# A two-block network on one core: latent norm moved forward, indexer slots in rotation, weight splits three ahead, a shorter inverse root, first gate group as whole fp32 products

## What is computed

```
h = rmsnorm(x, norm1_g[l])
z = h @ w_in[l]                                  # 2520 columns for four mixers, 4096 for gates
z_mla, z_nsa, z_fox, z_dsa, z_gate = split_cols(z, ...)
o_mla = mla_mixer(z_mla, ...)                    # starts with rmsnorm(c_q), rmsnorm(c_kv): the "latent" norm
o_nsa = nsa_mixer(...); o_fox = fox_mixer(...)
o_dsa = dsa_mixer(...)                           # an indexer scores all keys with 8 heads, top 64 are kept
lifted = einsum('bsnc,ncd->bsnd', stack(o_...), w_branch[l])
gates = sigmoid(z_gate)                          # 1024 -> 4 x 1024
x = x + sum(gates * lifted) @ w_out[l]
x = x + square(relu(rmsnorm(x) @ w_up[l])) @ w_down[l]
```

## Time and profile before

| | us |
|---|---|
| median of 3 runs | 1681.21 (1676.3 to 1685.93) |
| the profiled execution | 1678.43 |
| its span, first to last instruction | 1676.7 |
| TensorE busy | 1550.4 |
| VectorE, ScalarE, GpSimd busy | 821.7, 739.6, 595.2 |

### The profile page before, as it was taken

One profiled execution on the slowest core, in us unless ns is written; L12 is line 12 of the kernel. 1 busy time (PEld: TensorE's weight loads), 2 busy tenths in 40 slices (PEclk: granted clock), 3 DMA queues, 4 the chain that ended last, 5 costly groups with the idle time before them and its releaser, 6 DMA issues.

```text
span 1676.7 us, 23289 instructions
## 1 busy us (share of the span) xinstructions
PE 1550.4 (92%) x9590; PEld 1253.5 (75%) x9590; DVE 821.7 (49%) x1470; ACT 739.6 (44%) x1057; POOL 595.2 (35%) x227
## 2 busy tenths in 40 slices
PE   5999989999997999989889899999998798899997
PEld 4867867875996778578666658999886676589996
DVE  2734578324866764163664463522437733645222
ACT  3334366423436654143445344444434454354442
POOL 1200034320000442135555225655546443246543
PEclk9999889999997999999999999999999899999999
DMA  9597279769625786753343354555443333355550
GB/s 386 196 327 277 87 269 343 267 234 388 264 83 201 254 322 226 279 195 132 106 136 122 103 192 156 196 179 181 169 148 114 116 105 134 132 187 196 192 185 25
DMA packets 51225, 327.22 MB, mean 195 GB/s; under 512 B 5936, under 2 KB 5936, under 8 KB 17456
## 3 DMA queue, kind: packets, MB, share of 16 engines
q1 hardware_dynamic: 51120, 325.73, 53.8%
HBM read 324.66 MB, written 1.05 MB: 194 GB/s over the span
## 4 chain that ended last, share of the span: by engine, by line
PE 75%; DVE 17%; ACT 4%; DMA 2%; issue 1%; POOL 1%; DVEq 0%; SPq 0%; ACTq 0%
PE ps L224 19%; PE ps L225 18%; PE ps L226 18%; PE ps L221 16%; DVE lo L232 4%; DMA raw<-in_wmod 2%; DVE pb L2755 1%; PE ps L2704 1%; ACT hi L229 1%; DVE z L232 1%; DVE s L240 1%; ACT pb L229 1%; POOL lo L232 1%; DVE pb L232 1%; DVE rt L232 1%
## 5 line engine op out<-in xcount | busy, mean ns | idle before, releaser
L232 POOL TENSOR_TENSOR lo<-raw,hi 128x2048 fp32r<-128x2048 f32 (+2 forms) x76 | 354.2, 4670 | 647.4 <-ACT hi L229 647.4
L229 ACT ACTIVATE hi<-raw 128x2048 fp32r<-128x2048 f32 (+2 forms) x192 | 350.5, 1858 | 43.5 <-POOL big L232 16.9
L232 DVE TENSOR_TENSOR lo<-raw,hi 128x2048 fp32r<-128x2048 f32 (+1 forms) x116 | 291.8, 2531 | 97.1 <-ACT hi L229 96.9
L232 POOL TENSOR_TENSOR loh<-rawh,hih 128x1024 fp32r<-128x1024 f32 x64 | 156.0, 2450 | 141.9 <-ACT hih L229 141.6
L224 PE MATMUL ps<-hTh,hi 128*128 128x256 f32 x640 | 182.6, 285 | 5.4 <-DVE hTl L232 2.9
L225 PE MATMUL ps<-hTl,hi 128*128 128x256 f32 x640 | 181.8, 284 | 0.0
L226 PE MATMUL ps<-hTh,lo 128*128 128x256 f32 x640 | 181.7, 284 | 0.0
L224 PEld LDWEIGHTS ps<-hTh,hi 128*128 128x128 f32 x640 | 123.4, 193 | 7.2 <-issue 3.5
L224 PE MATMUL ps<-hi,hTh 128*128 128x512 f32 (+3 forms) x320 | 118.9, 372 | 10.2 <-DVE hTl L232 5.6
L225 PEld LDWEIGHTS ps<-hTl,hi 128*128 128x128 f32 x640 | 123.5, 193 | 0.5
L226 PEld LDWEIGHTS ps<-hTh,lo 128*128 128x128 f32 x640 | 123.5, 193 | 0.0
(11 more groups left out here) (306 smaller groups left out, 2990.1 us busy)
## 6 DMA issues: line engine op xcount, KB each, us to landing
raw<-in_wgu SPq DMA_DIRECT2D x64, 1024.0 KB, 4.9
raw<-in_wmod SPq DMA_DIRECT2D x48, 1024.0 KB, 6.9
raw<-in_wdn SPq DMA_DIRECT2D x32, 1024.0 KB, 5.6
rawh<-in_wgt SPq DMA_DIRECT2D x64, 512.0 KB, 3.8
raw<-in_wup SPq DMA_DIRECT2D x32, 1024.0 KB, 4.8
raw<-in_wdown SPq DMA_DIRECT2D x32, 1024.0 KB, 5.1
raw<-in_wz SPq DMA_DIRECT2D x12, 1024.0 KB, 4.7
raw<-in_wbr SPq DMA_DIRECT2D x8, 1024.0 KB, 4.9
```

The source lines that it names most:

```text
L229: return self.e.activation(o, a, f, **kw)
L232: return self.e.tensor_tensor(o, a, b, op)
```

## The change

Five edits, all in one diff. `v_fill` and `g_fill` change as `a_fill` does.

1. The first gate group (g = 0, four chunks per layer) is no longer split. TensorE multiplies the fp32 weights by the fp32 `hT` directly. The high slots in `hT`'s place become free when these are done.
2. The other gate chunks are split three ahead in place of two. The first two chunks of g = 1 are split at steps i = 1 and 2 of g = 0.
3. The first step of `v_latent` becomes `v_latent_in`, called in `v_indexer` before its first pause. It works in `s1` in place of `s2`.
4. The indexer's slot is `n % 4`, and ScalarE waits for head n - 4.
5. `v_rstd` takes one bit operation and one polynomial: 8 operations in place of 10. `v_stats`, which sums squares first, has them scaled in ScalarE's Square and takes 8 in all in place of 11.

```diff
     def enter_gates(self, l):
-        self.rings["H"] = [NH + i for i in range(4)]
+        self.rings["H"] = [NH + i for i in (2, 3, 0, 1)]
-        self.before["H"][NH:NH + 2] = [None] * 2
+        self.before["H"][NH:NH + 2] = [("used", ("gt", l, 0, 3))] * 2
...
     if name == "gt":
-        return part(t_in["wgt"][at[0], at[1]], at[2], 1024), "pool"
+        return part(t_in["wgt"][at[0], at[1]], at[2], 1024), "pool" if at[1] else "raw"
...
+    ROOT = 0.7235405817547222, -3.722988595072433, 5.6564527047170285, -4.5444396531968065, 2.4630066686385943
     def v_rstd(self, v, dst, ss, inv_n, tmp):
...
+        v.ts(dst.bitcast(I32), ss.bitcast(I32), -0.5, 1597463007.0, ALU.mult, ALU.add).then_inc(*v.up("dve"))
+        v.stt(tmp, dst, scale, dst, ALU.mult, ALU.mult).then_inc(*v.up("dve"))
         v.tt(tmp, tmp, ss, ALU.mult).then_inc(*v.up("dve"))
+        v.stt(ss, tmp, c[0], tmp, ALU.add, ALU.mult).then_inc(*v.up("dve"))
+        for x in c[1:3]:
+            v.stt(ss, ss, x, tmp, ALU.add, ALU.mult).then_inc(*v.up("dve"))
+        v.stt(dst, ss, c[3], dst, ALU.add, ALU.mult).then_inc(*v.up("dve"))
...
     def a_z(self, a, l):
-            if i == 5:
-                for k in range(4):
-                    a.wait_ge(*a.at("hT", ("c", l), k))
-                self.a_split(a, "gt", l, 0, 0, ahead=1)
...
     def t_fill(self, t, l):
                 c = t.chunk("gt", l, g, i)
+                if g:
+                    wh, wl = kn(c.hi, 2), kn(c.lo, 2)
+                    t.wait_ge(*t.at("lo", c.key))
+                else:
+                    t.wait_ge(*t.at("landed", c.key))
...
+                        else:
+                            m = t.mm(self.ps[:, b, :], self.hT[:, 2 * i + k, rows], kn(c.raw, 2)[:, k, :], first, last)
...
     def a_fill(self, a, l):
-                self.a_split(a, "gt", l, g, i, ahead=2)
+                if g:
+                    self.a_split(a, "gt", l, g, i, ahead=3)
+                elif i in (1, 2):
+                    self.a_split(a, "gt", l, 1, i - 1, ahead=0)
...
     def a_indexer(self, a, l):
-                        if n % 2:
-                            a.wait_ge(*a.at("idx head", l, n - 1))
-                        elif n >= 8:
-                            a.wait_ge(*a.at("idx head", l, n - 7))
+                        if n >= 4:
+                            a.wait_ge(*a.at("idx head", l, n - 4))
...
     def v_indexer(self, v, l):
         v.ts(V.wi, self.z[:, :, SM + 16:SM + 24], 8 ** -0.5, None, ALU.mult).then_inc(*v.up("dve"))
+        self.v_latent_in(v, l)
         yield
```

More of the change, by code:

```diff
@@ L101, in leave, with enter_gates @@
         self.before["H"][:NH - 1] = [key] * (NH - 1)
-    def enter_gates(self):
+    def enter_gates(self, l):
         self.epoch += 1
@@ L641, in v_gate @@
         v.mark("grow", l, g, half)
+    ROOT = 0.7235405817547222, -3.722988595072433, 5.6564527047170285, -4.5444396531968065, 2.4630066686385943
     def v_rstd(self, v, dst, ss, inv_n, tmp):
+        scale, *c = self.ROOT
         v.wait_ge(*v.last)
-        v.ts(ss, ss, inv_n, EPS, ALU.mult, ALU.add).then_inc(*v.up("dve"))
+        if inv_n is not None:
+            v.ts(ss, ss, inv_n, EPS, ALU.mult, ALU.add).then_inc(*v.up("dve"))
+            v.wait_ge(*v.last)
+        v.ts(dst.bitcast(I32), ss.bitcast(I32), -0.5, 1597463007.0, ALU.mult, ALU.add).then_inc(*v.up("dve"))
         v.wait_ge(*v.last)
[L650 to L654, removed]
+        v.stt(tmp, dst, scale, dst, ALU.mult, ALU.mult).then_inc(*v.up("dve"))
         v.wait_ge(*v.last)
@@ L657, in v_rstd @@
         v.wait_ge(*v.last)
-        v.stt(dst, tmp, 1.5, dst, ALU.add, ALU.mult).then_inc(*v.up("dve"))
-        c = 0.375 ** 0.5
+        v.stt(ss, tmp, c[0], tmp, ALU.add, ALU.mult).then_inc(*v.up("dve"))
+        for x in c[1:3]:
+            v.wait_ge(*v.last)
+            v.stt(ss, ss, x, tmp, ALU.add, ALU.mult).then_inc(*v.up("dve"))
         v.wait_ge(*v.last)
[L661 to L667, removed]
+        v.stt(dst, ss, c[3], dst, ALU.add, ALU.mult).then_inc(*v.up("dve"))
     def a_stats(self, a, name, src, ready, buf, c0, *freed, halves=(0, 1)):
@@ L676, in a_stats @@
                     a.wait_ge(*a.last)
-                a.ac(buf[:, 0:512], src[:, t, 512 * h:512 * h + 512], ACT.Square,
+                a.ac(buf[:, 0:512], src[:, t, 512 * h:512 * h + 512], ACT.Square, scale=1.0 / 32,
                      accum_out=self.st[:, c0 + 2 * h + t:c0 + 2 * h + t + 1]).then_inc(*a.up("act"))
@@ L684, in v_stats @@
         v.wait_ge(*v.at("squares", name))
-        v.tt(ss, ss, self.st[:, c0 + 2:c0 + 4], ALU.add).then_inc(*v.up("dve"))
-        self.v_rstd(v, self.st[:, c0 + 4:c0 + 6], ss, 1.0 / 1024, self.st[:, c0 + 6:c0 + 8])
+        v.stt(ss, ss, EPS, self.st[:, c0 + 2:c0 + 4], ALU.add, ALU.add).then_inc(*v.up("dve"))
+        self.v_rstd(v, self.st[:, c0 + 4:c0 + 6], ss, None, self.st[:, c0 + 6:c0 + 8])
         v.mark("rstd of", name)
@@ L2202, in t_fill @@
                     for k in range(2):
-                        m = t.mm3(self.ps[:, b, :], [h[:, 2 * i + k, 128 * q:128 * q + 128] for h in self.H3],
-                                  (wh[:, k, :], wl[:, k, :]), i == k == 0, i == 3 and k == 1)
+                        first, last, rows = i == k == 0, i == 3 and k == 1, slice(128 * q, 128 * q + 128)
+                        if g:
+                            m = t.mm3(self.ps[:, b, :], [h[:, 2 * i + k, rows] for h in self.H3],
+                                      (wh[:, k, :], wl[:, k, :]), first, last)
+                        else:
+                            m = t.mm(self.ps[:, b, :], self.hT[:, 2 * i + k, rows], kn(c.raw, 2)[:, k, :], first, last)
                     if i == 3:
@@ L2291, in v_fill @@
             for i in range(4):
-                self.v_split(v, "gt", l, g, i, ahead=2)
+                if g:
+                    self.v_split(v, "gt", l, g, i, ahead=3)
+                elif i in (1, 2):
+                    self.v_split(v, "gt", l, 1, i - 1, ahead=0)
                 yield
@@ L2331, in g_fill @@
             for i in range(4):
-                self.g_split(g, "gt", l, gg, i, ahead=2)
+                if gg:
+                    self.g_split(g, "gt", l, gg, i, ahead=3)
+                elif i in (1, 2):
+                    self.g_split(g, "gt", l, 1, i - 1, ahead=0)
                 yield
@@ L2439, in v_indexer @@
                         h = 4 * i + 2 * j2 + j
-                        r, wcol = s2[:, 256 * (h % 4):256 * (h % 4) + nk], V.wi[:, q, h:h + 1]
+                        r, wcol = s2[:, 256 * (n % 4):256 * (n % 4) + nk], V.wi[:, q, h:h + 1]
                         v.wait_ge(*v.at("idx relu", l, n))
@@ L2880, in a_latent, with v_latent_in @@
                      ps[0:96, b, :].rearrange("p (i n) -> p i n", i=2)).then_inc(*a.up(f"free{b}"))
-    def v_latent(self, v, l):
-        V, ps, st, s2 = self.views2(), self.ps, self.st, self.s2
+    def v_latent_in(self, v, l):
+        st, s1 = self.st, self.s1
         v.wait_ge(*v.empty("z", l, 3, 0))
@@ L2887, in v_latent @@
             v.wait_ge(*v.last)
-            v.tt(s2[:, 0:384], self.Z(t, ML, 384), self.Z(t, ML, 384), ALU.mult).then_inc(*v.up("dve"))
+            v.tt(s1[:, 0:384], self.Z(t, ML, 384), self.Z(t, ML, 384), ALU.mult).then_inc(*v.up("dve"))
             v.wait_ge(*v.last)
-            v.red(st[:, 8 + 2 * t:9 + 2 * t], s2[:, 0:256], ALU.add)
-            v.red(st[:, 9 + 2 * t:10 + 2 * t], s2[:, 256:384], ALU.add).then_inc(*v.up("dve"))
+            v.red(st[:, 8 + 2 * t:9 + 2 * t], s1[:, 0:256], ALU.add)
+            v.red(st[:, 9 + 2 * t:10 + 2 * t], s1[:, 256:384], ALU.add).then_inc(*v.up("dve"))
         v.wait_ge(*v.last)
@@ L2903, in v_latent @@
         self.v_rope(v, self.z[:, :, ML + 384:ML + 416].unsqueeze(2), 16, 0)
+    def v_latent(self, v, l):
+        V, ps = self.views2(), self.ps
         yield
@@ L3257, in tensor @@
             self.t_z(t, l)
-            t.book.enter_gates()
+            t.book.enter_gates(l)
             self.t_mixers(t, l)
```

7 lines of the change are left out of this document (2 added, 5 removed).

## The result

The changed kernel takes 1666.0 us in the median of five runs (1661.0 to 1666.7), beside 1676.3 us for the kernel before on the same chip: a ratio of 0.993 (95% interval 0.9911 to 0.9949), 10.3 us less. The prediction was 1657 us, twice that gain; the range held the result, and rival (a), at 1668 us, is nearer to it. The profiled execution took 1665.83 us with a span of 1664.1 us, 12.6 us less than in the earlier trace rows.

What follows compares the result with a forecast made beforehand. TensorE was taken as the bound, busy 1550.4 of 1676.7 us, all else costing only where it waits. Terms of -10.5 us (l = 0), -9.7 (l = 1) and the root sum to -21.4, giving 1657 us; range 1645 to 1674.

Steps and rivals of the forecast that it cites:

- rival (a): Smaller gain, chance 0.17: VectorE's chain stays the limit, savings return as waits at compressed probabilities and score banks; 1668 us.
- Whole products: First gate group: unsplit products cost 0.87 us against 0.68, +3.0 us per layer; rotation's wait goes, -1.96 per layer.
- Latent norm forward: Norm moved into VectorE's idle time before the indexer's heads: waits before the latent transposes go, -3.7 and -4.1 us.
- Slots in rotation: Indexer's relus and heads: gate bank wait goes, -2.2 and -1.9 us; compressed probabilities -0.5 us per layer.
- Splits three ahead: Gate chunks' low parts from GpSimd: four of five waits and half of the last go, -4.7 us in all.
- Shorter root: Norm b0 and the kernel's end lose three operations each, -1.2 us in all; other places hidden behind TensorE's products.
- The clock: TensorE's clock loss around the rotation's and latent norm's waits goes: -3.1 us in l = 0, -1.5 in l = 1.
- (c): Slower, chance 0.04: plain fp32 products do not overlap, 0.6 us or more per MATMUL; 1686 us or more.
- (d): Slower, chance 0.05: three ahead holds ScalarE before exponentials; a 2.7 us chunk at eight places, 21 us, takes all.

Runs made afterwards that it cites:

- the cut: Changed kernel with each gate low part on GpSimd as four subtractions of 256 columns in place of one of 1024; 1646.2 us, ratio 0.983.

## Why the prediction was right in sign and twice too large

That the time lies in the range is in part luck. The terms for the whole products and the root were too small by 8 and 3 us, and those for the slots, the splits three ahead and the latent norm too large by 5, 5 and 4.

**Whole products:** price and number right (0.86 us). Their worth was too small in the sum. With the rotation's 3.9 us and 1.7 us of clock it had them at +0.4 us, and the whole edit measured -7.8 us. In the changed kernel the low part that it removes stands beside a rotation that would wait 4.1 us per layer, not 1.96, with up to 5.0 us of clock.

**Latent norm forward:** right in place and mechanism. It ran at 792.9 to 802.6, one long block in it, no head late. The sum had -7.8 us and 2.9 of clock, measured were 6.7 us alone and 7.2 within the change. Alone, the wait and the clock behind it did go; what the sum lacks is what they turned into, 2.4 us more of low-part waits and a lower clock at 1320.

**Slots in rotation:** this step of the prediction failed. The step reads "-2.2 and -1.9 us" for the bank and "-0.5 us per layer" for the compressed probabilities, since "the heads end 0.9 us earlier". The bank wait did go, and the heads ended 1.2 us later (the first began 0.9 later) and the mask behind them 3 us: measured alone, the edit gains 7.4 us at bank and low parts and gives 7.4 back at the two waits behind the heads. The trace of before held the hint. ScalarE's 2.09 us in the earlier trace rows was read as lost time; the same pauses held back the rounding that sets GpSimd going. "TensorE also comes 0.9 us earlier, and blocks fall by chance" was the wrong sentence, as this order decides where they fall.

**Splits three ahead:** -4.7 us forecast, none measured (two ahead was 0.8 us faster). The waits went, but those of up to 1.1 us stood in front of a longer one (the forget gate's row), which took them over, and with three ahead that wait is 7.1 us in place of 4.6.

**Shorter root:** -1.2 us forecast, -4.5 measured. The two places of the sum, b0 and the end, gave the 0.6 us each; an odd layer's norm gave 0.5 more. I had priced the other norms as hidden and the clock around the routers not at all. How much is the clock's own scatter stays open: kernels that are the same instruction by instruction up to 780 us stand up to 4.0 us apart by 203 us in single profiles. The sign and size hold over it: at 700 us the ten profiles with the shorter root are 2.8 to 5.8 us ahead of the kernel before, and the other three with the old root within 0.8 us of it.

**The clock:** the sum took 4.6 us of it from the two mixers, and the change gave none in them (0.96 and 0.95 before, 0.95 and 0.95 after). Where the norm's wait went it rose, and around the two waits that grew it fell.

**The rivals:** (a) has the right size, 1668 us, and the right places (compressed probabilities, score banks), but its reason, that TensorE's savings return because VectorE paces, holds for part only: the early norm's saving does not return. The growth of its two waits comes from blocks that the slots brought. (c) and (d) showed nowhere.

The single effects (root 4.5, norm 7.2, whole products 7.8, three ahead none) add up to 19.5 us, and the change gives 10.3. The missing 9 us are the slots in company of the others, or how the edits overlap. The changed kernel without the slots alone was not run, so this split stays open. That GpSimd's blocks hold microseconds of this size is shown by the cut, which gives back 19.8 us with the same work in the same order; that they are these 9 is argued.

## What to carry to other kernels

Before a handshake between two engines is removed, look at what the pause holds back: here ScalarE's pause kept GpSimd quiet while VectorE ran its short operations. Where GpSimd and VectorE work beside each other, cut GpSimd's long instructions until a block is short, and try one step more of lead for the cut parts: here the lead gave nothing without the cut, and the cut 9 us without the lead and 20 with it. Do it only where GpSimd has time to spare. Price a wait of TensorE with the clock around it: with waits of 5.9 us cut to 2.4, about as much again came back between instructions that did not wait.

## What the runs showed of the hardware

- VectorE's operations with two inputs in SBUF stopped for what was left of a GpSimd low part, small ones too: 128 x 8 elements took 2.21 us beside a low part of 2.34 us, and 0.59 us beside quarters of 0.7 us. This is the rule of the Trainium skill (SBUF, Who interferes with whom), that the pair is held for a whole instruction, and the trace agrees. Some with one input were stopped too: the copy of 128 x 256 (2.42 us, else 0.28), the scaling of the first head before (2.49 us in the earlier trace rows, 0.35 after) and the operation of 128 x 4 in the earlier trace rows, 2.30 us. Maxima and replacements of 128 x 256 (0.43 and 0.41 us) had the same length with GpSimd busy and idle.
- GpSimd's four subtractions of 256 columns in a row took 2.77 to 2.92 us in the run with the cut, in place of 2.39 for one of 1024: 0.13 to 0.18 us for each additional instruction. In the stretch of twenty beside VectorE's heads it was 2.99 us for four.
- Two MATMULs of whole fp32 on 128 x 512 take 0.86 us at full clock, three passes of split operands 0.68.
- The granted clock was 0.83 in the mean over 820 to 860 us with waits of 5.9 and 3.1 us, and 1.00 with waits of 2.4 and 2.9 us over the same work. The length of a wait alone does not decide: in the kernel before, the rotation's wait of 1.96 us came with 0.88 (790 to 800 us) in l = 0, and the same wait with 1.00 (1255 to 1275 us) in l = 1.
